# Eight modulation blocks of layer 1 are summed by VectorE inside the first feed-forward instead of by TensorE

## The reference

```
for layer in range(2):
    mod   = silu(c)     @ ada_w[layer] + ada_b[layer]     # 1024 x 6144 weights
    mod_c = silu(c_ctx) @ ada_w[layer] + ada_b[layer]
    sh1, sc1, g1, sh2, sc2, g2 = split(mod, 6)            # the same six parts of mod_c
    ...
    x = x + g1 * mixer(rms_norm(x) * (1 + sc1) + sh1)
    x = x + g2 * conv_glu(rms_norm(x) * (1 + sc2) + sh2)
    if layer == 0: the same for ctx, with mod_c
conv_glu(h) = (silu(dwconv3(h @ w_up[:, :2816])) * (h @ w_up[:, 2816:])) @ w_down
```

## Time and profile before

| what | value |
|---|---|
| median of 3 runs | 2431.87 (2429.34 to 2434.84) |
| span of the profiled execution, first to last instruction | 2435.0 |
| first attention steps with their blocks | about 132 to 278 |
| first feed-forward, up part | 341.5 to 592.3 |
| first feed-forward, down part | 592.3 to 690 |

### The profile page before, as it was taken

How to read it: one execution, slowest core, us unless ns; L and a number is a source line. 1 busy time by engine, 2 the same in 40 slices (tenths; PEclk the granted TensorE clock), 3 DMA queues, 4 the chain that set the end, 5 groups by cost and what they waited for, 6 DMA issues and landing times.

```text
span 2435.0 us, 32307 instructions
## 1 busy us (share of the span) xinstructions
PE 2299.1 (94%) x13342; PEld 1514.5 (62%) x13342; DVE 949.6 (39%) x1584; ACT 747.7 (31%) x1113; POOL 69.3 (3%) x60
## 2 busy tenths in 40 slices
PE   5999899999999999999999899999999999999997
PEld 3944687787788899899798786333333333333332
DVE  4478543444143458666454655111111111111112
ACT  4366442333124433355345652111111111111101
POOL 0000000000000135000000000000000000000000
PEclk8999999999999999999999999999999999999999
DMA  9278135332222331245563168999999999999996
GB/s 347 70 277 242 35 122 197 115 104 104 87 104 70 104 105 36 90 153 176 187 220 127 54 181 345 398 428 428 429 428 429 428 429 428 429 428 429 428 429 289
DMA packets 142483, 603.14 MB, mean 248 GB/s; under 512 B 6720, under 2 KB 52032, under 8 KB 117664
## 3 DMA queue, kind: packets, MB, share of 16 engines
q1 hardware_dynamic: 142368, 601.52, 63.2%
HBM read 600.44 MB, written 1.05 MB: 247 GB/s over the span
## 4 chain that ended last, share of the span: by engine, by line
PE 76%; DMA 12%; DVE 5%; ACT 5%; issue 1%; POOL 0%; SPq 0%; DVEq 0%; ACTq 0%; POOLq 0%
PE bank L1054 74%; DMA arena<-in_w_up 5%; DMA ring<-in_w_up 5%; DMA ring<-in_ada_w 1%; PE bank L1281 1%; ACT arena L2387 1%; ACT w_high L2227 0%; DVE hw_low L2780 0%; ACT arena L2296 0%; ACT wide_p L2284 0%; PE bank L1702 0%; POOL arena L931 0%; DVE arena L2716 0%; DMA ring<-in_ffn_w_up 0%; ACT hw_high L2064 0%
## 5 line engine op out<-in xcount | busy, mean ns | idle before, releaser
L1054 PE MATMUL bank<-arena 128*64 128x512 f32 (+7 forms) x2256 | 442.1, 511 | 38.2 <-ACTq L792 21.6
L1054 PE MATMUL bank<-hT_high,w_split 128*128 128x512 f32 (+1 forms) x1408 | 345.7, 337 | 3.6 <-DVE hT_low L2458 3.6
L1054 PEld LDWEIGHTS bank<-arena 128*64 128x64 f32 (+2 forms) x2256 | 173.6, 156 | 275.2 <-issue 200.4
L1054 PE MATMUL bank<-ring,arena 128*64 128x512 f32 (+1 forms) x1248 | 301.5, 598 | 19.3 <-ACT arena L2387 11.8
L1054 PEld LDWEIGHTS bank<-hT_high,w_split 128*128 128x128 f32 x1408 | 242.1, 190 | 35.1 <-issue 4.1
L1054 PE MATMUL bank<-hT_low,w_split 128*128 128x512 f32 (+1 forms) x704 | 236.6, 336 | 0.0
L3156 DVE TENSOR_SCALAR arena<-bank 128x512 f32<-128x512 f32 x32 | 22.1, 692 | 542.6 <-PE bank L1054 542.4
L1054 PEld LDWEIGHTS bank<-ring,arena 128*64 128x64 f32 (+1 forms) x1248 | 99.9, 142 | 205.7 <-issue 182.3
L1054 PE MATMUL bank<-freed_w,arena 128*64 128x512 f32 x768 | 170.3, 595 | 6.0 <-ACT arena L2387 5.5
L1054 PEld LDWEIGHTS bank<-hT_low,w_split 128*128 128x128 f32 x704 | 133.6, 190 | 13.8 <-issue 0.2
L1054 PEld LDWEIGHTS bank<-freed_w,arena 128*64 128x64 f32 x768 | 53.4, 137 | 115.9 <-issue 104.2
(11 more groups left out here) (420 smaller groups left out, 3946.3 us busy)
## 6 DMA issues: line engine op xcount, KB each, us to landing
ring<-in_ada_w SPq DMA_DIRECT2D x24, 2048.0 KB, 8.3
ring<-in_w_gate SPq DMA_DIRECT2D x24, 2048.0 KB, 24.5
arena<-in_w_up SPq DMA_DIRECT2D x24, 2048.0 KB, 27.5
ring<-in_w_down SPq DMA_DIRECT2D x24, 2048.0 KB, 28.9
arena<-in_w_down SPq DMA_DIRECT2D x24, 2048.0 KB, 28.1
ring<-in_w_up SPq DMA_DIRECT2D x24, 2048.0 KB, 26.0
arena<-in_w_gate SPq DMA_DIRECT2D x24, 2048.0 KB, 25.1
ring<-in_ffn_w_up SPq DMA_DIRECT2D x42, 1024.0 KB, 7.8
```

What stands on the lines that cost most here:

```text
L1054: return pe.matmul(o, l, r, start=start, stop=stop)
```

## The change

The sixteen attention steps carry only twelve blocks: layer 0's 4 to 11 in steps 0 to 7 and layer 1's 0 to 3 in steps 8 to 11. Steps 12 to 15 carry none. `ADA_LATE` grows from four blocks to eight: 4, 5, 10, 11, 6, 7, 8, 9 of layer 1.

The eight late blocks are computed in another way. DVE multiplies each row group by its value of silu(c) and sums the eight groups into one half of `modp` (`ada_sum`): the first group with a tensor_scalar, the other seven with scalar_tensor_tensor, each 128x512. Four groups are done after `weights_low` at fc = 2j and four at fc = 2j+1. TensorE then only sums over partitions with a matrix of ones (`summed2`): four small matmuls for shift and scale, one of 512 columns for a gate. ACT's copy goes. A late block's slot is free when DVE has read its last group (`ada_summed`), where it was free after TensorE's matmuls before.

```diff
-        ADA_BETWEEN = [(0, 4 + i // 2) if i % 2 == 0 else (1, (0, 1, 2, 3, 6, 7, 8, 9)[i // 2]) for i in range(16)]
-        ADA_LATE = [4, 5, 10, 11]
+        ADA_BETWEEN = [*[(0, blk) for blk in range(4, 12)], *[(1, blk) for blk in range(4)]]
+        ADA_LATE = [4, 5, 10, 11, 6, 7, 8, 9]
...
+            elif key[0] == "ada" and unit_end[key] is None:
+                unit_done.append(("ada_summed", ADA_LATE.index(key[2]) + 1))
...
+            def summed2(blk):
+                await_next(ada_summed)
+                part = modp[:, ada_turn[1, blk], :]
+                if blk not in G_BLOCKS:
+                    key = ("adat", 1, blk)
+                    ps = bank(key)
+                    for i in range(4):
+                        m = mm(ps[:, 2 * i:2 * i + 2], part[:, i * P:(i + 1) * P], C("ones", 0, 2), True, True)
+                    close(m, key)
+                for row, v in gate_slots(1, blk):
+                    key = ("adag", 1, blk, row)
+                    close(mm(bank(key)[:, :], C("ones"), part, True, True), key)
...
-                    if l == 0 and 1 <= j < 5:
-                        ada2(1, ADA_LATE[j - 1])
-                    if l == 0 and j < 4:
-                        ada(1, ADA_LATE[j])
+                    if l == 0 and 1 <= j <= len(ADA_LATE):
+                        summed2(ADA_LATE[j - 1])
...
-                    if l == 0 and fc % 2 and fc < 8:
-                        ada(1, ADA_LATE[fc // 2])
...
+            def ada_sum(blk, half):
+
+                s, count = landed[unit_no["ada", 1, blk]]
+                if half == 0:
+                    dve.wait_ge(unit_landed[s], count)
+                w, acc = ring_col(s, 0, 512), modp[:, ada_turn[1, blk], :]
+                for k in range(4 * half, 4 * half + 4):
+                    if k == 0:
+                        do(dve.tensor_scalar(acc, w[:, k, :], cT[:, k, 0:1], None, ALU.mult))
+                    else:
+                        do(STT(out=acc, in0=w[:, k, :], scalar=cT[:, k, 0:1], in1=acc, op0=ALU.mult, op1=ALU.add),
+                           ada_summed if k == KC - 1 else dve_step)
...
                     if fc + 2 < FC:
                         weights_low(l, fc + 2)
-                    if l == 0 and fc % 2 and 2 < fc < 10:
+                    if l == 0 and fc < 2 * len(ADA_LATE):
+                        ada_sum(ADA_LATE[fc // 2], fc % 2)
+                    if l == 0 and fc % 2 and 2 < fc < 2 * len(ADA_LATE) + 2:
                         ada2(1, ADA_LATE[fc // 2 - 1])
```

More of the change, by code:

```diff
@@ L387, in plan_ada @@
             col_unit(("ada", l, blk), a["ada_w"][l], blk * 512)
-            add(("adap", l, blk), "act")
         def plan_ada2(l, blk):
@@ L511, in program @@
                     add(("probt", t, g, c), "dve" if c else "act")
-            if i < len(ATT0):
+            if i < len(ADA_BETWEEN):
                 l, blk = ADA_BETWEEN[i]
@@ L520, in program @@
                 add(("pv", t, g), "dve")
-            if i < len(ATT0):
+            if i < len(ADA_BETWEEN):
                 plan_ada2(l, blk)
-                if i in WO_AFTER:
-                    out_unit(WO_AFTER[i])
+            if i in WO_AFTER:
+                out_unit(WO_AFTER[i])
         def plan_pair(tag, v):
@@ L550, in plan_ffn @@
                     add(("val", l, 2 * j + i), "dve")
-                if l == 0 and 1 <= j < 5:
+                if l == 0 and 1 <= j <= len(ADA_LATE):
                     plan_ada2(1, ADA_LATE[j - 1])
-                if l == 0 and j < 4:
+                if l == 0 and j < len(ADA_LATE):
                     plan_ada(1, ADA_LATE[j])
@@ L647, in program @@
             if key[0] == "ada":
-                unit_end[key] = ("adap", *key[1:])
+                unit_end[key] = ("adap", *key[1:]) if ("adap", *key[1:]) in group else None
             elif key[0] == "up":
@@ L724, in program @@
         x_high, x_low = sem("input_high"), sem("input_low")
-        SEM = {"psum_ready": psum_ready, "units_used": units_used, "w_low": w_low_v}
+        ada_summed = sem("ada_summed")
+        SEM = {"psum_ready": psum_ready, "units_used": units_used, "w_low": w_low_v, "ada_summed": ada_summed}
         freed = {"act": sem("freed_by_act"), "dve": sem("freed_by_dve")}
@@ L1300, in _ @@
                 if i > 1:
-                    weighted(i - 2, lambda i=i: ada(*ADA_BETWEEN[i]) if i < len(ATT0) else None)
-                if i < len(ATT0):
+                    weighted(i - 2, lambda i=i: ada(*ADA_BETWEEN[i]) if i < len(ADA_BETWEEN) else None)
+                if i < len(ADA_BETWEEN):
                     ada2(*ADA_BETWEEN[i])
```

## The result

The changed kernel takes 2474.57 us (median of 4 runs, 2474.0 to 2477.47) against 2430.61 for the kernel before on the same chip. The ratio is 1.0175, 95% interval 1.0159 to 1.0191: 44.0 us slower. Its profiled execution spans 2475.4, where the prediction's sum was 2476.0.

A forecast was written before the change was run, and what follows sets the result against it. PE bounds the up part now; afterwards a loop through DVE's sums and queued loads would. 2435.0 - 3.6 + 43.1 + 2.5 - 1.0 = 2476.0 profiled, so 2473 predicted; range 2447 to 2494, about 0.84.

The forecast's parts named there:

- The loop: First feed-forward's up part: splits, sums and two queued loads take 29.7 us per two feature chunks; PE needs 22.8.
- the trip of 15.7: Up part: from ACT's split of a landed up block to SP's next modulation block issue, 15.7 us.
- X of 14.0: Up part: from the modulation block's issue until both it and the up block behind have landed; range 8.26 to 15.14 us.
- VectorE's price: DVE's sums in the up part: 752 ns per scalar_tensor_tensor, 486 for the first; 6.06 us per block, 48 in all.
- 2.5 of clock: Up part: lower PE clock after a wait costs 2.5 us, counted only after the last wait.
- the rival of a clock lost at every wait: Up part: PE's slow stretches are not taken from the next waits, 15 us more, 2488; chance 0.06.
- The small first wait: Up part: PE waits 1.7 us for up block 2, before the six waits of 6.9.
- near 0.5: Sign of being right: windows show a granted clock near 0.5 after PE's seven waits in the up part.
- TensorE's savings: First feed-forward: four blocks' matmuls and gate sums removed (11.8 us), eight partition sums added (8.2); gain 3.6 us.
- Attention: Attention steps: 2.9 us gained in emptied steps, 1.9 lost to two more gate blocks; net gain 1.0 us.
- a gain of 2.9: Attention steps 12 to 14: PE's first products start earlier without a block, by 0.6, 1.4 and 0.9 us.
- the loop's own range: Whole time if the loop holds, with X, sum price, attention and clock varied: 2446 to 2499 us; the loop's chance 0.78.

The follow-up runs named there:

- The two reordered kernels: Changed kernel with each late modulation block queued behind the next up block: 2438.11 us with eight late blocks, 2433.7 with four and attention as before.
- the reordered kernel: Changed kernel, eight late blocks, each late modulation block queued behind the next up block instead of ahead: 2438.11 us against 2432.38, ratio 1.0032.
- filler: Changed kernel with three repeats of four overwritten transposes on TensorE in attention steps 12 to 15: 2477.91 us against 2429.2, ratio 1.0195.

## Why the prediction was right

**The loop.** Right, step by step: the trip of 15.7 measured 15.69, X of 14.0 measured 13.9 to 14.9, the loop of 29.7 measured 30.0. Two runs changed one term each, and the loop moved by it: half the sums 26.8, half the load 27.1. A third kept all the work and put the sums in another place: 24.2. The two reordered kernels kept the work too and removed the dependence, and PE's waits were gone. That DVE as a busy engine is not the cause is shown by the reordered kernel with 151.3 us of DVE and a full PE.

**VectorE's price.** The sums ran at 752 ns, the row chosen from the earlier trace rows, and at 487 for the first group:

```profile
L2498 DVE SCALAR_TENSOR_TENSOR modp<-ring,cT,modp 128x512 f32<-128x512 f32 x56 | 42.1, 752 | 2.0
L2496 DVE TENSOR_SCALAR modp<-ring,cT 128x512 f32<-128x512 f32 x8 | 3.9, 487 | 0.3
```

The 691 ns of the Trainium skill (VectorE: DVE Perf Modes, errata section) are for another operation, a tensor_tensor. The trace of the kernel before agrees there, with 692 ns for most tensor_tensors of this size that read SBUF alone, but the sums run as the row of their own operation.

**Waits and clock.** Six waits of 6.9 and one of 1.7 were predicted, 43.1 us, and 2.5 of clock. Seven of 33.0 in all came, and PE was busy 262.9 - 247.1 = 15.8 us longer with the same work at a lower clock. Together that is 48.8 against 45.6: the loop sets the pace and the slow matmuls fill the waits, as the prediction said, so the rival of a clock lost at every wait on top fell. The 3.2 us more come mostly from the six loops being 30.0 and not 29.7 (2.0). The small first wait was 1.80 (1.7 predicted). The granted clock in the 6 us behind the seven waits was 0.51 to 0.72, so "near 0.5" held for the second and the last only. Behind the last wait, the one whose loss counts, it was 0.53, 2.8 us (2.5 predicted). The Trainium skill (TensorE: Matmul & The Clock Gate, HAM oscillation) describes bursts that start at the low clock after a wait for a load. The trace agrees for the six waits of 4.1 to 6.0 us, whose first matmuls run at the low level; behind the wait of 1.80 the first five matmuls still run at the high one. The 2488 of that rival didn't come, because each slow stretch lies in time that PE would have waited.

**TensorE's savings.** 3.6 predicted, 4.5 measured where nothing waits. The up part as a whole: +42.0 predicted, +44.3 measured.

**Attention: the term that was mis-sized.** Predicted -1.0, measured +2.9. The last block that both kernels multiply in attention, step 11's, splits it; before and after:

```profile
210.60 1.92 PE L1054 MATMUL bank<-ring,cT 128*32 128x512 f32 x16
211.52 1.92 PE L1056 MATMUL bank<-ring,cT 128*32 128x512 f32 x16
```

Up to here the changed kernel has lost 2.3 us: this block starts 86.0 after the last query projection instead of 83.8. Of these, 2.1 come between the blocks of steps 6 and 8, where the two more gate blocks lie (1.9 predicted). From here to the output projection a gain of 2.9 was predicted, and 0.6 was lost (68.9 against 68.3). The first parts of the gain came. Step 12's product starts 97.03 after the last query projection instead of 95.31, so 0.55 of the 2.3 is made good (0.6 predicted), and step 13 comes another 1.16 earlier (231.96 - 222.51 against 232.74 - 222.13; 1.4 predicted). But from step 12 to step 16 it takes 1.15 longer (45.23 against 44.08), so 2.3 are lost in steps 14 to 16, because PE, now waiting for ACT, falls to the lower clock. I had put the clock in at the one wait of the earlier trace rows and not at the waits that the change makes.

Six more profiles with the steps emptied and no filler show the same term at either clock. In three the first of the three windows still has a clock of 1.00: step 13 to 14 takes 9.13 us, as with filler, and the stretch from step 11's block is 0.5 to 0.6 shorter than before. In the other three, as in the changed kernel, the clock is 0.83 there, step 13 to 14 takes 10.3 to 10.6, and the stretch is 0.5 to 0.9 longer. So emptying the steps was worth between 0.6 gained and 0.9 lost, never 2.9. Attention as a whole took 152.5 to 152.7 in the former and 154.8 to 155.2 in the latter. About half of that distance is older than the emptied steps: step 1's block starts 13.8 to 14.1 us after the last query projection in the former and 15.1 in the latter, and both values occur in kernels with a block in every step too; what decides it stays open. That the clock fell because the steps were emptied is what the filler shows: in the second window it is 0.83 in all seven profiles without it, and 1.00 with it and with the blocks.

The total came out closer than its terms, which is luck: +2.3 (up part) and +3.9 (attention) against -6.8 in stretches that the change doesn't touch, of which -4.4 after the up part. Between the medians 41.1 were predicted and 44.0 measured. The lower end of the loop's own range adds up to 2445, not 2446; nothing hangs on it.

## What to carry to other kernels

When work moves from a full engine to one with idle time, don't ask first whether that time suffices; ask which buffer the work now holds, what stands behind that buffer's reload in an in-order queue, and whether the trip from one landing to the next issue, plus the landing, is still shorter than the full engine's period. If it is not, put the urgent load ahead of the one that frees late, or gather the work so that its buffer frees early: either gave back some 36 us here with the work unchanged. When you reorder loads in a ring, compare the slots of every later unit too.

## What the runs showed of the hardware that was not expected

Taking 3 to 4 us of matmuls (1.92 and 1.05 or 1.98) out of each of four attention steps, where ScalarE was about to set the pace, lowered TensorE's granted clock in those steps in all seven profiles without filler, in four from step 13 on and in three from step 14 on, from 1.00 to 0.83 and then 0.70 to 0.75, already behind waits of 2.2 us. Twelve transposes per step, 1.47 us, held it at 1.00 until step 15, in the one profile with filler.

Two loads of 2 MB issued 0.47 us apart took 14 us until the second was usable; 3 MB took 11.1, and one alone 8.3. So a load is made late by the bytes that stand ahead of it in the queue, even if they are wanted later.
